# The MLP up projection of a two-layer decoder trunk as a stage of its own, with seven block products in place of eight

## The reference

```python
def squared_relu_mlp(h, w_up, w_down):
    return jnp.square(jax.nn.relu(h @ w_up)) @ w_down

for i in range(DEPTH):
    h = rmsnorm(x, norm_mix[i])
    x = x + mixer_i(h)                       # retention (i = 0), sliding-window attention (i = 1)
    h = rmsnorm(x, norm_mlp[i])
    x = x + squared_relu_mlp(h, w_up[i], w_down[i])
```

## Time and profile before

| | us |
|---|---|
| median of three runs | 2750.98 |
| the profiled execution, its own time | 2752.24 |
| its span, first to last instruction | 2750.4 |
| PE busy | 2658.4 (97%) |
| DVE busy | 1572.6 (57%) |
| ACT busy | 746.5 (27%) |
| POOL busy | 477.9 (17%) |

### The profile page before, as it was taken

One profiled execution on the slowest core, in us unless ns is written; L12 is line 12 of the kernel. 1 busy time (PEld: TensorE's weight loads), 2 busy tenths in 40 slices (PEclk: granted clock), 3 DMA queues, 4 the chain that ended last, 5 costly groups with the idle time before them and its releaser, 6 DMA issues.

```text
span 2750.4 us, 35656 instructions
## 1 busy us (share of the span) xinstructions
PE 2658.4 (97%) x12273; PEld 2216.8 (81%) x12273; DVE 1572.6 (57%) x3049; ACT 746.5 (27%) x1400; POOL 477.9 (17%) x473
## 2 busy tenths in 40 slices
PE   8999999999999999999999988999979999999999
PEld 6878878788788788888888877888868888888887
DVE  7554454544677644544445488888875444454443
ACT  6232222322313211111111255555551111111112
POOL 2102011020001211111111153323331111111010
PEclk9999999999999999999999999999999999999999
DMA  6012120121432111111111101001011111111111
GB/s 201 27 47 69 47 74 12 47 65 51 149 97 87 39 54 46 46 46 48 59 46 46 38 23 39 17 24 39 32 31 46 46 46 60 46 46 46 46 46 61
DMA packets 124795, 146.67 MB, mean 53 GB/s; under 512 B 15729, under 2 KB 97937, under 8 KB 124690
## 3 DMA queue, kind: packets, MB, share of 16 engines
q1 hardware_dynamic: 122386, 141.14, 16.4%
q10 hardware_dynamic: 2304, 4.20, 0.4%
HBM read 128.54 MB, written 16.78 MB: 53 GB/s over the span
## 4 chain that ended last, share of the span: by engine, by line
PE 80%; DVE 11%; issue 5%; ACT 3%; POOL 0%; DVEq 0%; DMA 0%; ACTq 0%; SPq 0%; POOLq 0%
PE ps L420 26%; PE ps L422 26%; PE ps L421 25%; ACT xn L1460 1%; DVE xT L597 1%; DVE hT_lo L465 1%; DVE wqg_lo L387 1%; DVE smax L1507 1%; PE ps L858 1%; DVE pT_lo L1484 1%; PE ps L859 1%; PE ps L860 1%; DVE hss L1540 1%; PE ps L906 0%; PE ps L890 0%
## 5 line engine op out<-in xcount | busy, mean ns | idle before, releaser
L597 DVE TENSOR_TENSOR xT<-ps,xT 128x512 f32<-128x512 f32 x704 | 475.0, 689 | 273.7 <-PE ps L422 273.7
L420 PE MATMUL ps<-aT_hi,wd_hi 128*128 128x512 f32 x1408 | 555.2, 394 | 7.9 <-DVE xT L597 4.9
L421 PE MATMUL ps<-aT_lo,wd_hi 128*128 128x512 f32 x1408 | 550.3, 391 | 0.0
L422 PE MATMUL ps<-aT_hi,wd_lo 128*128 128x512 f32 x1408 | 550.2, 391 | 0.0
L420 PE MATMUL ps<-hT_hi,wu_hi 128*128 128x512 f32 x1024 | 401.1, 392 | 0.0
L422 PE MATMUL ps<-hT_hi,wu_lo 128*128 128x512 f32 x1024 | 399.1, 390 | 0.0
L421 PE MATMUL ps<-hT_lo,wu_hi 128*128 128x512 f32 x1024 | 399.1, 390 | 0.0
L694 POOL TENSOR_TENSOR sqr_t<-relu_t 128x512 f32<-128x512 f32 x128 | 188.1, 1470 | 1168.8 <-DVE relu_t L702 1168.8
L420 PEld LDWEIGHTS ps<-aT_hi,wd_hi 128*128 128x128 f32 x1408 | 265.8, 189 | 63.3 <-DVE xT L597 5.8
L422 PEld LDWEIGHTS ps<-aT_hi,wd_lo 128*128 128x128 f32 x1408 | 265.7, 189 | 55.9
L421 PEld LDWEIGHTS ps<-aT_lo,wd_hi 128*128 128x128 f32 x1408 | 266.0, 189 | 53.8
(11 more groups left out here) (255 smaller groups left out, 4333.4 us busy)
## 6 DMA issues: line engine op xcount, KB each, us to landing
raw<-in_w_up SPq DMA_DIRECT2D x64, 512.0 KB, 3.9
raw<-in_w_down SPq DMA_DIRECT2D x64, 512.0 KB, 3.3
raw<-in_ret_w_in SPq DMA_DIRECT2D x48, 512.0 KB, 4.7
y_dram<-xn SPq DMA_DIRECT2D x32, 256.0 KB, 2.3
raw<-y_dram SPq DMA_DIRECT2D x16, 512.0 KB, 3.2
raw<-in_ret_w_out SPq DMA_DIRECT2D x16, 512.0 KB, 3.4
xtok<-in_x SPq DMA_DIRECT2D x8, 512.0 KB, 5.9
xT<-x_dram SPq DMA_DIRECT2D x8, 512.0 KB, 7.5
```

The lines of the kernel that those rows point to most:

```text
L420: pe.matmul(bank, ah, bh, start=(i == 0), stop=False)
L421: pe.matmul(bank, ah, bl, start=False, stop=False)
L422: last = pe.matmul(bank, al, bh, start=False, stop=(i == len(pairs) - 1))
L597: dve.tensor_tensor(xT[:, k, cols], ps[:, banks[m % len(banks)], :], xT[:, k, cols], ALU.add).then_inc(x_add, 1)
```

## The change

The MLP of each layer becomes two stages: all of the up projection, whose squared results go to a new DRAM tensor `a_dram`, and then all of the down projection, which reads them back. The up projection works on 8 pairs of groups. In a pair, h is taken as 2 x 2 blocks (halves of K by halves of the tokens) and the weights as 2 x 2 blocks (halves of K by two 128-wide blocks of hidden features), twice (q = 0, 1). Seven products of 4 blocks of K (12 matmuls) form the four results, 14 products in a pair. The seven combinations of h (bh, bl) are formed and split once in each layer, at its start; the sums of weight blocks (8 of 128 x 512 in a pair) are formed by POOL in `u_sum`, ahead of ACT's and DVE's splits. Banks 4 and 5 take products 1, 6 and 7 on top of each other, and ACT copies them out between. The square is ACT's alone. The down stage splits both the activations and the weights of a group from loaded pieces, one group ahead, as the retention output projection does.

In the edge, the norm's factor is found for both halves at once, after all squares. The x that the combinations were formed from is saved in `x_dram` and read back before the down stage, since bh, bl take its place in SBUF.

The core of the diff:

```diff
+ORDER = {True: (1, 2, 5, 6, 4, 7, 3), False: (1, 6, 4, 7, 2, 5, 3)}   # True: the first pair of a layer
+U_BANK = {1: 4, 6: 4, 7: 4, 2: 0, 5: 2, 3: 2, 4: 6}
+URING = 7
+        def u_load_next(sp, layer, p, first):
+            g = PAIRS * layer + p
+            for j in range(4):
+                sp.wait_ge(u_lo, OPS * g + op_pos(first, 7 if j < 2 else 3, j % 2) + 1)
+                u_load(sp, layer, p + 1, j)
+        def u_sum(eng, layer, p, first, i, q):
...
+            if i == 5:
+                arrived(eng, PC_U[layer], p, 4, q)
+                arrived(eng, PC_U[layer], p, 4, 2 + q)
+                wait(eng, u_lo, OPS * g)
+                eng.tensor_tensor(us1[:, q, :, :], weight(7, q), weight(4, q), ALU.add).then_inc(s_set, 1)
...
+        def u_pe(pe, layer, p, first, between=lambda s: None):
...
+                if i == 6:
+                    pe.wait_ge(u_cp, 6 * g + 1 + q)
+                if i == 7:
+                    pe.wait_ge(u_cp, 6 * g + 3 + q)
+                if i == 3:
+                    pe.wait_ge(u_add, 8 * g + c_pos(first, 22, q) + 1)
+                product(pe, ps[:, U_BANK[i] + q, :],
+                        [(uw_hi[:, s % URING, k * P:(k + 1) * P], uw_lo[:, s % URING, k * P:(k + 1) * P],
+                          bh[i][:, k, :], bl[i][:, k, :]) for k in range(4)], begin=i in (1, 2, 4, 5)).then_inc(u_mm, 1)
...
+        def u_dve(dve, layer, p, ahead):
+            for s in range(OPS):
+                for c, q in results_of(s):
+                    u_add_dve(dve, layer, p, False, c, q)
+                if s + URING < OPS:
+                    u_lo_dve(dve, layer, p, False, s + URING)
+                else:
+                    ahead(s)
+                for c, q in results_of(s):
+                    u_relu_dve(dve, layer, p, False, c, q)
...
+        def edge_act(act, layer, m, final):
+            if m < 4:
+                b_hi_act(act, layer, 1, m, final)
+            elif m < KT:
+                b_hi_act(act, layer, 2, m - 4, final)
+            elif m < 12:
+                h12_act(act, layer, m - KT, final)
+            else:
+                b_hi_act(act, layer, 3, m - 12, final)
+            norm_square(act, 2 * layer + 1, m)
+            if m >= 12:
+                b_hi_act(act, layer, 5, m - 12, final)
+        def edge_dve(dve, layer, final):
+            for i in (0, 1):
+                u_lo_dve(dve, layer, 0, True, 4 + i)
+            for kk in range(4):
+                t_dve(dve, layer, 6, kk, final)
+            for kk in range(4):
+                b_lo_dve(dve, layer, 6, kk)
+            norm_rstd(dve, 2 * layer + 1, 0)
+            dve.wait_ge(n_rsq, RSQ * (RS_AT[2 * layer + 1] + 1))
+            for half in range(2):
+                norm_dg(dve, 2 * layer + 1, half)
+            for i in (0, 1):
+                u_lo_dve(dve, layer, 0, True, 6 + i)
...
+            for i in (0, 1):
+                u_lo_dve(dve, layer, 0, True, 12 + i)
+            for s in (7, 8, 9):
+                next_lo(dve, layer, 0, s)
+            for s in (10, 11):
+                for c in (22, 21):
+                    u_add_dve(dve, layer, 0, True, c, s - 10)
+                next_lo(dve, layer, 0, s)
...
+        def first_pair_pe(pe, layer, final):
+            def between(s):
+                if s == 1:
+                    norm_stat_pe(pe, n, 0)
+                    pe.wait_ge(x_add, final + TILES)
+                if s == 3:
+                    for half in range(2):
+                        norm_rb_pe(pe, n, half)
...
+        def up_sp(sp, layer, final):
+            for m in range(TILES):
+                x_save(sp, m, final)
+            for c, q in RESULTS[True][:2]:
+                u_store(sp, layer, 0, True, c, q)
+            u_load_next(sp, layer, 0, True)
...
+            for kind in ("m1", "u2", "u3", "e"):
+                for q in range(2):
+                    sp.wait_ge(a_out[kind, q], 16 * PAIRS * (layer + 1))
+        def down_sp(sp, layer):
+            for j in range(4):
+                dn_load(sp, layer, 1, j)
+        def dn_dve(dve, layer, g, b):
+            for m in range(TILES):
...
+                add(dve, DG_D[layer] + g, m)
+                if m % 4 == 0:
+                    dn_lo_dve(dve, layer, g + 1, m // 4, b)
```

The end of the retention output projection on DVE, before and after:

```diff
-            finish_dve(dve, RET_GROUPS - 1, 1, lambda m: mlp_up_lo(dve, 0, PC_M0) if m == 1 else None)
+            for m in range(TILES):
+                add(dve, RET_GROUPS - 1, m)
+                if m < 2:
+                    u_lo_dve(dve, 0, 0, True, m)
+                if 2 <= m < 10:
+                    edge_low(dve, 0, m - 2)
+                if m in (10, 11):
+                    u_lo_dve(dve, 0, 0, True, m - 8)
+                if 9 <= m < 13:
+                    t_dve(dve, 0, 5, m - 9, final)
+                if m >= 12:
+                    b_lo_dve(dve, 0, 5, m - 12)
+            edge_dve(dve, 0, final)
```

More of the change, by code:

```diff
@@ new lines, in u_hi_act @@
+        def u_hi_act(act, layer, p, first, s):
+            i, q = op_at(first, s)
+            g = PAIRS * layer + p
+            wait(act, u_mm, OPS * g + s - URING + 1)
+            if i in (1, 2, 4):
+                arrived(act, PC_U[layer], p, 4, q if i == 1 else 2 + q)
+            else:
+                act.wait_ge(s_set, 8 * g + SUM_AT[first][i, q])
+            if layer == 1 and first and s == 5:
+                act.wait_ge(n_ss, sums(3, 1, KT - 1))
+            act.activation(uw_hi[:, s % URING, :].rearrange("p (k n) -> p k n", n=P), weight(i, q),
+                           ACT.Copy).then_inc(u_hi, 1)
@@ new lines, in u_dve, with next_hi @@
+        def u_dve(dve, layer, p, ahead):
+            for s in range(OPS):
+                for c, q in results_of(s):
+                    u_add_dve(dve, layer, p, False, c, q)
+                if s + URING < OPS:
+                    u_lo_dve(dve, layer, p, False, s + URING)
+                else:
+                    ahead(s)
+                for c, q in results_of(s):
+                    u_relu_dve(dve, layer, p, False, c, q)
+        def next_hi(act, layer, p, s):
+            u_hi_act(act, layer, p + 1, False, s + URING - OPS)
@@ new lines, in first_pair_pool, with up_pool @@
+        def first_pair_pool(pool, layer, final):
+            pool.wait_ge(down_mm, final + TILES)
+            for q in range(2):
+                u_sum(pool, layer, 0, True, 5, q)
+            for q in range(2):
+                u_sum(pool, layer, 0, True, 7, q)
+                u_sum(pool, layer, 0, True, 6, q)
+            for q in range(2):
+                u_sum(pool, layer, 0, True, 3, q)
+        def up_pool(pool, layer):
+            with pool.Fori(1, PAIRS) as p:
+                for q in range(2):
+                    for i in (5, 7, 6):
+                        u_sum(pool, layer, p, False, i, q)
+                for q in range(2):
+                    u_sum(pool, layer, p, False, 3, q)
@@ new lines, in down_act @@
+        def down_act(act, layer, after):
+            for j in range(4):
+                dn_hi_act(act, layer, 1, j, 1)
+            after()
+            with act.Fori(1, MLP_GROUPS // 2) as gg:
+                for b in range(2):
+                    for j in range(4):
+                        dn_hi_act(act, layer, 2 * gg + b, j, D_BUF[b])
+        def dn_dve(dve, layer, g, b):
+            for m in range(TILES):
+                if isinstance(g, int) and g == 0 and m < KT:
+                    dve.wait_ge(x_in_s[m], 16 * (3 + layer))
+                add(dve, DG_D[layer] + g, m)
+                if m % 4 == 0:
+                    dn_lo_dve(dve, layer, g + 1, m // 4, b)
@@ new lines, in down_dve @@
+        def down_dve(dve, layer, last_adds):
+            dn_dve(dve, layer, 0, 1)
+            with dve.Fori(0, MLP_GROUPS // 2 - 1) as gg:
+                dn_dve(dve, layer, 2 * gg + 1, 2)
+                dn_dve(dve, layer, 2 * gg + 2, 1)
+            last_adds()
+        def down_sp(sp, layer):
+            for j in range(4):
+                dn_load(sp, layer, 1, j)
+            with sp.Fori(2, MLP_GROUPS) as g:
+                for j in range(4):
+                    dn_load(sp, layer, g, j)
```

950 lines of the change are left out of this document (597 added, 353 removed).

## The result

Five runs of the kernel after gave 2763.11 to 2770.09 us, median 2766.88; the kernel before gave 2753.11 beside it. The ratio is 1.0055, with a 95% interval of 1.004 to 1.0069: slower by half a per cent, where 2731 and faster had been forecast. The profiled execution has a span of 2767.9 and a time of its own of 2770.09, 17.9 above that of before.

What follows compares the result with a forecast made beforehand. PE's matmuls were taken to bound the MLP; -87.1 + 3 + 25.6 + 26.3 + 12.4 + 0.3 = -19.5 from the profiled 2752.24 gave 2732.7, or 2731 as median, with a range of 2704 to 2758 us.

Steps and rivals of the forecast that it cites:

- The matmuls: Up projection: 24 fewer matmuls in each of 16 pairs, at 0.2267 us each: -87.1 us.
- The steady pair: Up projection's later pairs: PE needs 38.1 us; POOL's sums cost PE 0.2 in each of 14 pairs: +3, bounds 0 and 22.
- the price of DVE beside POOL: DVE operations with both inputs in SBUF: counted at 1.10 us while POOL works, 0.60 otherwise.
- The rival of POOL's sums: Steady pairs: POOL's chain of sums makes product 12 wait 1.6 us a pair, junctions cost 66: 2765 us; chance 0.14.
- the prediction's own signs: Steady pairs: 38.1 to 38.5 us would show it right; over 39.5 would mean POOL's chain.
- The junction of layer 0: From last projection group into first up pair: 34.1 us lost against 8.5, +25.6.
- (a): Layer 0's junction: DVE's tiles and combinations, then rounds with ACT for tiles 12 to 15, until 913.
- (b): Layer 0's junction: first weight sum, ten DVE operations beside POOL and the norm; PE gets factors at about 929.
- Step (d): Layer 0's junction: third weight load lands at 954.7, then sums and splits; addition 22, awaited by PE's product 12, at 961.4.
- layer 1: Layer 1's junction into its first up pair: 39.8 us lost against 13.5, +26.3.
- From up to down: Between up and down stages, twice: PE waits 4.3 us for store, load and splits, plus 1.9 slow clock: +12.4.
- Others: Last group of layer 0's MLP: two more 1024-wide weight splits on DVE, +0.3; down groups' DVE work hidden.

Runs made afterwards that it cites:

- run 2: Kernel after, POOL's sums of weight blocks for the steady pairs cut to 2 of 128 columns: 2743.66 us, ratio to before 0.9969.
- run 11: Kernel after, steady-pair splits before squares, down projection's splits late, POOL's sum 7 late, first pair's additions and ACT's copies earlier: 2705.6 us, ratio to before 0.9832.
- run 6: Kernel after, in steady pairs ACT makes the next product's split before squaring the last result: 2754.03 us, ratio to before 1.001.
- run 3: Kernel after, sums cut to 2 of 128 columns, each followed by a full POOL addition on an unused buffer: 2748.54 us, ratio to before 0.9994.
- run 4: Kernel after, only the second block's sums of each steady pair cut to 2 of 128 columns: 2750.79 us, ratio to before 0.9997.
- run 1: Kernel after, steady pairs' weight sums formed by DVE in place of POOL, pair 1's left with POOL: 2765.76 us, ratio to before 1.0052.
- run 8: Kernel after, first pair's DVE additions put ahead of most of the next pair's splits, ACT's squares likewise: 2755.24 us, ratio to before 1.0011.
- run 7: Kernel after, DVE's four activation splits for the second down group moved behind tiles 6, 8, 10, 12 of the first: 2748.81 us, ratio to before 0.9992.
- run 5: Kernel after, POOL's sum 7 of both blocks moved last, behind the previous pair's last addition 22: 2770.34 us, ratio to before 1.0071.
- run 9: Kernel after, at the junction DVE makes the norm's root and diagonal factors before product 6's table and splits: 2766.73 us.

## Why the prediction was wrong

**The matmuls** were right: 384 fewer, 38.08 us a pair wherever nothing waits (runs 2 and 11).

**The steady pair** is the step that failed: "I take 0.2 for each of 14 pairs", +3 forecast, +20.4 measured. That is 17.4 of the 37.4 us between the forecast's -19.5 and the 17.9 of the profiled executions, the largest part. Of the 20.4, 17.1 are in the twelve pairs beside POOL's sums. Two things in the step were wrong.

The first is the price of DVE beside POOL. It was counted at 1.10, after the 1.18 of the earlier trace rows, where an addition out of PSUM stood ahead of the split and let a part of POOL's operation pass. Where POOL's has only just begun, DVE waits for nearly all of it: 1.78, and POOL's own 1.30 became up to 1.84. The kind of sum is not the reason: in run 6, beside the same sums, the splits behind an addition took 1.18 again. The trace of before had dear ones too, in the attention drain, beside POOL's sums of squares. Timeline of DVE, kernel before:

```profile
2020.43 1.68 DVE L465 SCALAR_TENSOR_TENSOR hT_lo<-xT,gT,hT_hi 128x512 fp32r<-128x512 f32 x1
...
2028.19 1.70 DVE L465 SCALAR_TENSOR_TENSOR hT_lo<-xT,gT,hT_hi 128x512 fp32r<-128x512 f32 x1
```

The second is the path. I tested only one chain, that of POOL's sums, against its due time. It was met: the third sum ended 7.3 us after the copy of product 6 (1111.91), ACT took it 4.7 later, and in run 2, where nothing is delayed, ACT takes it 8.8 after the copy, still 1.5 later. The bound was the round between DVE and ACT that every product goes through. The rows for it were there: DVE's 0.60 twice, ACT's square and split, 2.51 in all against 2.72. I added DVE's operations up to 18 to 22 of 38 us and called nothing full, though a round with 0.21 to spare can make good 3 us of delay only over 15 products, and a pair has 14. Run 2 shows that the sums cause the wait, runs 3 and 4 that it grows with the time DVE loses beside POOL, run 1 that work of DVE's own does the same without POOL, and runs 6 and 11 that the loop is what turns this time into a wait.

The other 3.3 us, at the end of layer 0's last pair, stand beside tables and wider splits on DVE, for which the prediction had no term. They stay without the sums (3.4 in run 2) and shrink to 0.5 with the loop opened (run 6), which points at the same loop.

**The rival of POOL's sums** named 2765, and the kernel came to 2767; its place, product 12, and its 1.4 to 1.6 us a pair were nearly right as well (1.34 in twelve pairs). Its mechanism was not: no split waited for a sum in the steady pairs. That its total fits is in part luck: junctions of 60.2 where it had 66, but 24.4 for the hand-overs and the rest where it had 12.7, and 3.3 of the steady pairs' 20.4 are not POOL's. It was given 0.14. Neither of the prediction's own signs, 38.1 to 38.5 or over 39.5 us a pair, came up: most pairs took 39.4.

**The junction of layer 0**: steps (a) and (b) gave factors at 929, the scale matmuls started at 930.37. The price of DVE was wrong here too (four combinations took 6.86 where 4.4 was counted), but it cost little: DVE's ten operations in (b) took 12.9 in place of 11. Step (d) had addition 22 at 961.4, and product 12 started at 966.58, 5.2 late. Most of that is in the loads. SP issues four of 512 KB within 2.1 us, and ACT splits the first of them only 5.6 us after its issue. The third was counted with 3.9 and landed after 7.3 (952.72 to 960.03), so POOL began its sums at 960.25 in place of 954.7. The sums themselves took 1.26 each, less than counted. Timelines of DVE, SP and ACT:

```profile
917.21 6.86 DVE L904 SCALAR_TENSOR_TENSOR ut<-xT,gT,ut 128x512 f32<-128x512 f32 x4
951.59 2.12 SPq L683 DMA_DIRECT2D raw<-in_w_up  x4
957.18 0.63 ACT L719 ACTIVATE uw_hi<-raw 128x512 fp32r<-128x512 f32 x1 [6.13 <-DMA raw<-in_w_up]
```

That `next_lo` ahead of addition 22 holds PE is confirmed by run 8. In layer 1, +29.5 for +26.3, the third load landed after 6.6.

**From up to down**: the wait was 6.2 where 4.3 was forecast, and the lower clock cost 2.2 to 2.5 where 1.9 was. The mechanism was right, as run 7 confirms: ACT's split waits for the load of what the last store wrote, DVE's split waits for ACT, and the addition behind it holds PE's bank. Timelines of SP, ACT and DVE:

```profile
1256.15 1.66 SPq L699 DMA_DIRECT2D a_dram<-xn  x2
1259.69 0.82 SPq L418 DMA_DIRECT2D raw<-a_dram  x2
1263.50 1.06 ACT L425 ACTIVATE aT_hi<-raw 128x1024 fp32r<-128x1024 f32 x1 [6.11 <-DMA raw<-a_dram]
1264.59 1.22 DVE L432 TENSOR_TENSOR aT_lo<-raw,aT_hi 128x1024 fp32r<-128x1024 f32 x1 [7.27 <-ACT aT_hi L425]
1265.73 2.48 DVE L645 TENSOR_TENSOR xT<-ps,xT 128x512 f32<-128x512 f32 x4
```

The forecast had the first addition behind the split end 11.1 after the last product (1252.46), at 1263.6; its row gives 1265.73 + 0.6 = 1266.3, 2.7 late. The lateness is in front: the first row holds two stores, and the second, the last of the stage, was issued at 1257.5, 5.0 after the last product where 2.0 had been counted, because DVE's relus stood behind the tables. The load was issued 2.2 after it and ACT's split began 3.8 later, both as counted. In layer 1 the last store was issued 3.0 after the last product, but the load only 3.9 behind the store.

**Others**: +0.3 forecast for the weight splits in layer 0's last group. Some 4 us in layer 1's attention had not been foreseen, and no run looked for their cause.

The range (2704 to 2758) ended 9 us short. The prediction had the dearer case, 22 for the steady pairs together with 66 for the junctions, as a rival at 2765, and left this part out of the range. The steady pairs' 20.4 and the junctions' 60.2 lay within their own bounds, the hand-overs' 18.2 just above theirs, and only the rest, 6.2 for 0.3, had no bound at all.

## What to carry to other kernels

An engine's busy share says nothing about a loop between two engines: write down the round that one unit of work makes through both, and compare it with the time of that unit on the bounding engine. What is left over is the rate at which a delay is made good. Where GpSimd takes over elementwise work, price the VectorE operations beside it first, each by what is left of GpSimd's operation when it begins, then the sums themselves; and look at what stands ahead of a producer in program order, since moving a wait gave nothing (runs 5 and 9) or half of what was hoped (run 8) until the next instruction in line was moved too.

## What was not expected of the hardware

- A 128x512 operation of DVE with both inputs in SBUF takes turns with an operation of POOL's: begun while POOL's runs, it ended 0.55 us after it, 37 times of 37 in the steady pairs of the kernel after and 72 of 72 in run 6. So it took 0.69 alone and up to 1.78 beside a POOL sum of two inputs (1.30 alone), and 1.40 in run 3 beside a POOL addition of one buffer to itself (1.04 alone). POOL's took up to 1.84 and 1.48 where DVE's had begun first. DVE's additions out of PSUM kept 0.68 beside either. The Trainium skill, GPSIMD Engine Reference, "Key points", tells of the contention for instructions with two SBUF inputs; the trace agrees, and shows the price: up to 1.09 us more for each operation, where 0.50 had been assumed.
- After pauses of 6 to 10 us PE's matmuls were 0.43 apart, 1.2 GHz, for 9 to 12 matmuls (the granted clock from 1266 to 1272 is 0.59); after the pauses of about 1 us before product 12 only the first one was longer (0.50 for 0.39). After a pause of 2.4 us at the start of layer 1's junction both were seen, a first matmul of 0.80 in the kernel after and of 0.50 in run 7.
